# A transformer stack in float32 on one core: x, tables and results kept feature-major, modulation summed by VectorE

## What is computed

```python
for i in range(2):                                   # first block
    x = x + 0.5 * swiglu(rms_norm(x, g[i, 0]), w_gate_up[i, 0], w_down[i, 0])
    x = x + attention_i(rms_norm(x, g[i, 1]))
    x = x + 0.5 * swiglu(rms_norm(x, g[i, 2]), w_gate_up[i, 1], w_down[i, 1])
for i in range(2):                                   # second block
    shift_x, scale_x, gate_x = split(silu(c) @ w_mod[i] + b_mod[i], 3)
    shift_c, scale_c, gate_c = split(silu(c_ctx) @ w_mod[i] + b_mod[i], 3)
    hx = rms_norm(x, norm_g[i]) * (1 + scale_x) + shift_x
    hc = rms_norm(ctx, norm_g[i]) * (1 + scale_c) + shift_c
    ox, oc = mixer_i(hx, hc)
    x = x + gate_x * (ox @ w_o[i])
    if i == 0: ctx = ctx + gate_c * (oc @ w_o[i])
return rms_norm(x, final_g)
```

## Time and profile before

| | us |
|---|---|
| median of 3 runs (lowest, highest) | 3031.51 (3030.82, 3036.52) |
| the profiled execution, its own time | 3030.34 |
| its span, first to last instruction | 3028.5 |
| mean granted TensorE clock, of full speed | 0.972 |
| TensorE matmul busy | 2870.4 |
| VectorE / ScalarE / GpSimd busy | 1529.5 / 1147.8 / 110.4 |
| moved by DMA | 234.27 MB, 77 GB/s over the span |

### The profile page before, as it was taken

How to read it: one execution, slowest core, us unless ns; L and a number is a source line. 1 busy time by engine, 2 the same in 40 slices (tenths; PEclk the granted TensorE clock), 3 DMA queues, 4 the chain that set the end, 5 groups by cost and what they waited for, 6 DMA issues and landing times.

```text
span 3028.5 us, 38808 instructions
## 1 busy us (share of the span) xinstructions
PE 2870.4 (95%) x14416; PEld 2334.9 (77%) x14416; DVE 1529.5 (51%) x2151; ACT 1147.8 (38%) x1799; POOL 110.4 (4%) x108
## 2 busy tenths in 40 slices
PE   7999999998999999999987899999999997999987
PEld 2588888887888888888866788887788886878876
DVE  2244426665544335442456444424566666367774
ACT  2323215555323224222354332223455555245452
POOL 1000000000000000000011000000101000010100
PEclk9999999999999999999998899999999998999998
DMA  8433322122333233333301133332111110111111
GB/s 306 153 93 99 99 97 60 45 62 56 98 97 97 97 97 88 99 93 103 92 28 29 49 94 101 91 105 75 49 42 42 35 42 21 56 42 29 43 29 63
DMA packets 333666, 234.27 MB, mean 77 GB/s; under 512 B 6952, under 2 KB 308112, under 8 KB 333584
## 3 DMA queue, kind: packets, MB, share of 16 engines
q1 hardware_dynamic: 332672, 231.63, 25.4%
q0 software_dynamic: 912, 1.53, 0.2%
HBM read 231.04 MB, written 2.10 MB: 77 GB/s over the span
## 4 chain that ended last, share of the span: by engine, by line
PE 88%; DVE 5%; ACT 4%; issue 2%; DMA 0%; POOL 0%; ACTq 0%; SPq 0%; DVEq 0%; POOLq 0%
PE ps L439 24%; PE ps L441 24%; PE ps L440 23%; PE ps L732 3%; PE ps L708 2%; PE ps L1067 2%; PE ps L1204 2%; PE ps L956 1%; PE ps L1042 1%; ACT apr L1837 1%; PE ps L835 1%; PE ps L839 1%; PE ps L920 1%; PE ps L1184 1%; DVE tmp L488 1%
## 5 line engine op out<-in xcount | busy, mean ns | idle before, releaser
L439 PE MATMUL ps<-act_h,wl 128*128 128x512 f32 x2224 | 891.5, 401 | 3.6 <-DVE act_l L2037 2.3
L441 PE MATMUL ps<-act_h,wh 128*128 128x512 f32 x2224 | 868.1, 390 | 0.0
L440 PE MATMUL ps<-act_l,wh 128*128 128x512 f32 x2224 | 867.3, 390 | 0.0
L434 DVE TENSOR_TENSOR wl<-raw,wh 128x1024 fp32r<-128x1024 f32 x382 | 461.1, 1227 | 526.5 <-ACT wh L430 521.7
L430 ACT ACTIVATE wh<-raw 128x1024 fp32r<-128x1024 f32 x382 | 392.5, 1051 | 420.8 <-PE ps L441 347.8
L439 PEld LDWEIGHTS ps<-act_h,wl 128*128 128x128 f32 x2224 | 418.7, 188 | 96.1 <-issue 10.6
L440 PEld LDWEIGHTS ps<-act_l,wh 128*128 128x128 f32 x2224 | 419.1, 188 | 89.9 <-issue 7.9
L441 PEld LDWEIGHTS ps<-act_h,wh 128*128 128x128 f32 x2224 | 418.2, 188 | 89.4
L439 PE MATMUL ps<-h_h,wl 128*128 (+1 forms) x704 | 277.4, 394 | 0.0
L441 PE MATMUL ps<-h_h,wh 128*128 (+1 forms) x704 | 276.0, 392 | 0.0
L440 PE MATMUL ps<-h_l,wh 128*128 (+1 forms) x704 | 273.2, 388 | 0.0
(11 more groups left out here) (339 smaller groups left out, 3805.7 us busy)
## 6 DMA issues: line engine op xcount, KB each, us to landing
raw<-in_ffn_w_gate_up SPq DMA_DIRECT2D x176, 512.0 KB, 4.0
raw<-in_ffn_w_down SPq DMA_DIRECT2D x88, 512.0 KB, 3.7
mod_raw<-in_w_mod SPq DMA_DIRECT2D x12, 2048.0 KB, 8.0
raw<-in_a_w_in SPq DMA_DIRECT2D x32, 512.0 KB, 4.1
raw<-in_sb_w_in SPq DMA_DIRECT2D x24, 512.0 KB, 3.9
raw<-in_b_w_in SPq DMA_DIRECT2D x20, 512.0 KB, 4.0
raw<-in_w_o SPq DMA_DIRECT2D x16, 512.0 KB, 4.0
raw<-in_sw_w_in SPq DMA_DIRECT2D x10, 512.0 KB, 4.0
```

The lines of the kernel that those rows point to most:

```text
L434: dve.tensor_tensor(wl[:, slot, :], raw[:, slot % RAWS, :], f32(wh[:, slot, :]), ALU.subtract).then_inc(lo_done[slot], 1)
L439: pe.matmul(bank, w_lo, r_hi, start=start, stop=False, skip_group_check=skip)
L440: pe.matmul(bank, w_hi, r_lo, start=False, stop=False, skip_group_check=skip)
L441: return pe.matmul(bank, w_hi, r_hi, start=False, stop=stop, skip_group_check=skip)
```

## The change

All transposes at the two ends go, by laying the arrays out on the host.

- x and ctx come feature-major, one contiguous 2 KB run for each partition and tile. SP issues first one DMA for `columns` (128 x 430: gains, b_mod, sinks, lambda vectors, frequencies), then the eight tiles of x, `kf`, `krows`, and then the FFN weights. The setup stage's transposes, copies, zeroing and the 17 small DMAs are gone.
- Each engine's work for the first tiles stands in `first_norm`: split of slot 0, then act_h/act_l tile by tile as x lands, split of slot 1, squares of x, the copy of `kr`.
- The mod stage is gone. w_mod comes as 96 chunks of 128 x 512 (output feature on the partition, half of the 1024 inputs along the row), issued on GpSimd's queue into two buffers (one of them in xc's space). GpSimd's queue also loads silu's arguments, broadcast to all partitions. For each chunk DVE runs two tensor_tensor_reduce (multiply, sum along the row), one for c and one for c_ctx, into `mpart`. 48 chunks are summed in each of the first two FFNs: 3 in each pass of the gate/up loop from the second on, 1 behind each of 18 `split_lo` of the down projection. DVE's loops of those two FFNs are unrolled. ACT takes the silu of the broadcast rows in the first pass of each.
- Lambda and the other small constants are worked out between the two loops of the first FFN (`constants` on DVE, `lambda_exponentials` on ACT), and `modulation` (7 small operations) at the same place of the fourth FFN.
- ctx is loaded by GpSimd's queue after the last chunk; its sum of squares is formed in the out stage of sw.
- At the end each of the eight tiles of `yt` is stored by its own 256 KB DMA on SP's queue as soon as it is written; the transposes and copies are gone.

Of the two functions named `first_norm` below, the first is ScalarE's, the second VectorE's; `modulation` is GpSimd's, `modulated` and `two` are VectorE's.

```diff
         def _(sp):
+            sp.dma_start(columns[:, :], a["columns"]).then_inc(columns_in, 16)
+            for k in range(KT):
+                sp.dma_start(x[:, k, :], a["x"][:, k, :]).then_inc(x_in[k], 16)
+            sp.dma_start(kf[:, :], a["shape_table"][:, 0:N_F * P]).then_inc(const_in, 16)
+            sp.dma_start(krows, a["shape_table"][:, N_F * P:]).then_inc(const_in, 16)
...
-            sp.wait_ge(rows_out, 8)
-            sp.dma_start(y_out[0].rearrange("(b p) d -> p b d", p=P), yrows[:, :, :]).then_inc(out_sem, 16)
-            sp.wait_ge(out_sem, 16)
+            for k in range(KT):
+                sp.wait_ge(xf_done, START + 8 * stages[-2].n["xf"] + k + 1)
+                sp.dma_start(y_out[:, k, :], yt[:, k, :]).then_inc(out_sem, 16)
+            sp.wait_ge(out_sem, 16 * KT)
...
+            def modulation(half_):
+                pool.wait_ge(mod_used, START + half_ * MOD_CHUNKS // 2)
+                for v, name in enumerate(("c_2", "c_ctx_2")):
+                    pool.dma_start(mod_silu[:, v, :], a[name][:, half_ * SEQ:(half_ + 1) * SEQ].to_broadcast([P, SEQ])
+                                   ).then_inc(mod_row_in, 16)
+                for i in range(half_ * MOD_CHUNKS // 2, (half_ + 1) * MOD_CHUNKS // 2):
+                    if i > 1:
+                        pool.wait_ge(mod_used, START + i - 1)
+                    pool.dma_start(mod_w[i % 2], a["w_mod_2"][:, i, :]).then_inc(mod_in[i % 2], 16)
...
+            def first_norm(st):
+                split_hi(act, *half(st.following, 0))
+                for k in range(KT):
+                    act.wait_ge(x_in[k], 16)
+                    act.activation(act_h[:, k, :], x[:, k, :], ACT.Identity,
+                                   scale=vec[:, st.gain + k:st.gain + k + 1]).then_inc(xhi_done, 1)
+                split_hi(act, *half(st.following, 1))
+                for n in range(KT):
+                    square(act, stages[0], n)
+                act.wait_ge(const_in, 16 * 2)
+                act.activation(kr[:, :, :].rearrange("p a b -> p (a b)"), krows, ACT.Copy).then_inc(consts_done, 1)
...
+            def first_norm(st):
+                split_lo(dve, *half(st.following, 0))
+                for k in range(KT):
+                    dve.wait_ge(x_in[k], 16)
+                    dve.nop().then_inc(xup_done, 1)
+                    gained_lo(st, k)
+                split_lo(dve, *half(st.following, 1))
+                for n in range(KT):
+                    add_square(dve, stages[0], n)
+                dve.wait_ge(consts_done, 2)
...
+                def modulated(n):
+                    i = f * MOD_CHUNKS // 2 + n
+                    if n == 0:
+                        dve.wait_ge(mod_silu_done, f + 1)
+                    dve.wait_ge(mod_in[i % 2], 16 * (i // 2 + 1))
+                    dve.wait_ge(mod_used, START + i)
+                    for v in range(2):
+                        last = dve.tensor_tensor_reduce(mod_w[i % 2] if v else mod_prod, mod_w[i % 2], mod_silu[:, v, :],
+                                                        1.0, 0.0, ALU.mult, ALU.add, mpart[:, f, n, v:v + 1])
+                    last.then_inc(mod_used, 1)
+
+                def two(i, extra):
                     split_lo(dve, *half(st, 2, i))
                     split_lo(dve, *half(st, 3, i))
                     gate_scaled(0, i)
                     up_scaled(0, i)
+                    if extra:
+                        modulated(3 * i - 3)
                     gated(0, i)
                     split_lo(dve, *half(st, 4, i))
                     h_lo(0, i)
+                    if extra:
+                        modulated(3 * i - 2)
                     gate_scaled(1, i)
                     split_lo(dve, *half(st, 5, i))
                     up_scaled(1, i)
+                    if extra:
+                        modulated(3 * i - 1)
                     gated(1, i)
                     h_lo(1, i)
...
+                if f == 0:
+                    constants()
+                if f == 3:
+                    modulation()
+                if f < 2:
+                    for t in range(2, 24):
+                        split_lo(dve, *half(st, 2 * FT + t))
+                        if t < 20:
+                            modulated(28 + t)
```

More of the change, by code:

```diff
@@ L167, in ffn @@
         plan.stage("ffn", lead=2 * FT + FT, layer=layer, j=j, count=("ffn", "res"))
-    plan.stage("setup", count=("res", "cres"))
-    plan.stage("mod")
+    plan.stage("setup", count=("res",))
     ffn(0, 0)
@@ L178, in make_plan @@
     plan.stage("sw", lead=2, fixed=2, times=4)
-    plan.stage("out", lead=8, w="sw", count=("res",))
+    plan.stage("out", lead=8, w="sw", count=("res", "cres"))
     ffn(1, 1)
@@ L215, in build_program @@
     w_down = [[tiled(a["ffn_w_down"][l, j]) for j in range(2)] for l in range(2)]
-    w_mod = [tiled(a["w_mod_2"][l]) for l in range(2)]
     w_sb_in, w_sw_in = tiled(a["sb_w_in"][0]), tiled(a["sw_w_in"][0])
@@ L665, in _ @@
                         pool.memset(f32(t[:, :, :]), 0.0).then_inc(B.zero, 1)
+                if st.kind == "ffn" and st.n["ffn"] < 2:
+                    modulation(st.n["ffn"])
                 if st.kind == "sw":
@@ L1320, in out_projection @@
                                 ctx_args=(ps[:, 4 + t, 0:CTX], actc_h, actc_l) if st.ctx else None)
-            def end():
-                pe.wait_ge(xf_done, START + 8 * stages[-1].before["xf"])
-                for b in range(NBLK):
-                    for k4 in range(2):
-                        transposes(2 * b + k4, lambda k: yt[:, 4 * k4 + k, b * P:(b + 1) * P],
-                                   4).then_inc(etr_done, 1)
-            for st in stages:
-                if st.kind == "setup":
-                    setup()
-                elif st.kind == "mod":
-                    modulation(st)
-                elif st.kind == "norm":
+            for st in stages:
+                if st.kind == "norm":
                     norm(st)
@@ L1400, in norm @@
                     if st.before["res"] == 1:
[L1401 to L1402 removed]
+                        first_norm(st)
                     return
@@ L1430, in norm @@
                         act.activation(dst[:, k, :], src, ACT.Copy).then_inc(xhi_done, 1)
-            def modulation(st):
-                for n in range(MOD_LOADS):
-                    act.wait_ge(mod_used, START + n + 1)
-                    act.activation(mod_rows[0:2, n * SEQ:(n + 1) * SEQ], ps[0:2, 2 + n % 4, :],
-                                   ACT.Copy).then_inc(mod_copied, 1)
-                for t in range(2):
-                    split_hi(act, *half(st, t))
             def ffn(st):
@@ L2042, in norm @@
                     if st.before["res"] == 1:
-                        for k in range(KT):
-                            gained_lo(st, k)
+                        first_norm(st)
                     return
```

284 lines of the change are left out of this document (119 added, 165 removed).

## The result

The changed kernel takes 2943.88 us (median of 4 runs, 2934.53 to 2944.93), the kernel before 3034.02 beside it on the same chip (3030.82 to 3038.26). The ratio is 0.9695, with a 95% interval of 0.9671 to 0.972: faster by 90 us. The prediction was 2924.4 with a range of 2918 to 2935. It was **wrong**: the sign and most of the gain are there, but the kernel is 19.5 us slower than forecast. Two later executions, one with a spacer of 192 bytes (3273.92 us at a granted clock of 0.83) and one of the kernel before beside it (11497.76 us), lay far outside all others and stand in no ratio.

What follows compares the result with a forecast made beforehand. TensorE's matmuls bound the middle, so only the two ends could gain: 3028.5 - 98.0 - 10.4 + 0.8 + 0.5 = 2921.4 us of span, 2923.2 profiled, 2924.4 as median; range 2918 to 2935.

Steps and rivals of the forecast that it cites:

- The first matmul: Start: TensorE's first projection begins at 17.65 us (15.6 to 19.7) instead of 115.67, 98.0 us less.
- the first rival: Start: raw 0 shares the rate or x lands late; first matmul at 20 to 22, time 2927 to 2931; chance 0.11.
- The third term, from landing to matmul: Start: ACT's and DVE's splits, then gained_lo to the first matmul, 1.07, 1.18 and 0.90, together 3.15 us.
- The clock at the start: First projection: the same 6 us at 1.2 GHz as before, no difference in time.
- The mean: First norm: mean of squares ready 11.7 us behind the first matmul, mean 0.1 later; 0.8 us more (0 to 2).
- VectorE's work and the chunks: First two FFNs: 192 sums of 0.7 us, 134 us hidden; chunks land in 4 us against 9.6; nothing on the path.
- The second and third rivals: First two FFNs: chunks land late, 2930 to 2949 us, chance 0.09; slow sums make VectorE the bound, 192 t - 387, chance 0.02.
- The rule of the shared port: GpSimd's queue: VectorE in a port-sharing mode blocks GpSimd's DMA descriptors; chunks could land several us late, against 9.6 us allowed.
- Constants behind the loop: Between the first FFN's loops: constants and exponentials delay the slots' splits, 11.8 against 11.0; 0.5 us more (0 to 3), once.
- The middle of the kernel: From first L439 to last yt: the prediction is wrong if this is longer than 2899.1 + 1.3 us.
- The median: Whole kernel: median of the runs 1.2 us above the profiled execution, 2923.2 to 2924.4.
- The end: Last norm and stores: the end comes at 3018.1 on the old timeline instead of 3028.5, 10.4 us less.

Runs made afterwards that it cites:

- spacer of 192 bytes: Kernel before with 192 unused bytes a partition ahead of the overlaid tensors (h_h at 138112): 3028.5 us, ratio 0.9987.
- The early load: Changed kernel with ScalarE's first table load asked for before its first wait: 2943.22 us, ratio 0.971.
- The spacers: Unused tensors ahead of the overlaid ones: kernel before with 32, 64, 192 bytes, 3044.28, 3048.27, 3028.5 us; changed kernel with 32, 160 bytes, 2926.57, 2945.24 us.
- The 32 bytes: Changed kernel with an unused tensor of 32 bytes a partition ahead of the overlaid tensors (h_h at 138624): 2926.57 us, ratio 0.9651.
- the same bytes in the kernel before: Kernel before with the 32-byte unused tensor ahead of the overlaid tensors (h_h at 137952): 3044.28 us, ratio 1.0045.
- the 64 bytes: Kernel before with 64 unused bytes a partition ahead of the overlaid tensors (h_h at 137984): 3048.27 us, ratio 1.0037.

## Why the prediction was wrong, and where it was right

**The first matmul (17.65, 15.6 to 19.7): mis-sized.** It came at 23.55. In kind this is the first rival, a late start because raw 0 shares the rate, but it came beyond even that rival's 20 to 22. Two terms failed. Raw 0 landed at 19.06, not at 14.5: I had summed the rates of the kernel before to 4.67 MB, but those belonged to another queue. In the changed kernel the same sum over its own rates reaches 4.67 MB only at 16.7 us, and raw 0 lands 2.3 later, while raw 1 shares the rate. GpSimd's queue did not begin at about 5 us as I read from the earlier trace rows, where its first issue had waited for VectorE, but at 2.40, and had issued its megabyte by 4.7. Holding GpSimd back gave 3.2 of these 4.6 us; for the rest the low rate from 3 to 6 us remains, cause open. Second, "ACT's first table load, and columns, come long before" was half wrong: columns did, but the table load stood behind the wait for raw 0, for 1.28 us. The early load moved it to 3.24 and showed this. The third term, from landing to matmul, was right: 3.15 forecast, 23.55 - 20.35 = 3.20 measured. The sum is 4.6 + 1.3 + 0.05 = 5.9 us.

**The clock at the start.** I expected 6 us of slow matmuls. They took 0.63 us each until 27.1 and 0.40 from then, 3.6 us behind the first. It was worth nothing, since the mean waits for the squares, not for TensorE. The record of the granted clock shows 1.00 in these 3.6 us, where the earlier trace rows show 0.50; the durations are the better witness here.

**The mean (+0.8): right.** 35.2 is 11.65 behind the first matmul, forecast 11.8.

**VectorE's work and the chunks: right.** A sum takes 685 ns (forecast 0.7), with another starting 0.61 us later; chunks landed in a median of 3.3 us (forecast 4) and GpSimd waited for VectorE, never VectorE for a chunk. Only the first two took as long as the sign of being wrong (9.6 and 10.0 us, in the crowded start); they were first used at 61.5 and cost nothing, and of the others none took over 7.7. No TensorE wait in the first two FFNs but the mean's, 1.6 us. Leaving the work out changed 0.5 us of the total. The second and third rivals did not happen; the third's price was tested with four times the sums: its place and its waits held (114 us), and its sum fell 34 us or more short of the 165 measured, for want of the slower clock.

**The rule of the shared port.** The transfers of w_mod were issued from GpSimd's queue in 0.54 us each, all 96 alike, and landed in 3.3 us in the median while VectorE was busy 209.5 of the first FFN's 364.2 us. The Trainium skill, SBUF — State Buffer, in its part on the two sides of SBUF, gives the slowing for VectorE's faster modes; the trace agrees that float32 products and sums don't bring it about, and no run here shows the other case.

**Constants behind the loop (+0.5): nothing.** Lambda and its exponentials ended at 273.5 and the slots were split by 277.7; TensorE had no wait there. The estimate of 0 to 3 held its lower end.

**"The middle of the kernel" (2899.1 + 1.3 us): this step failed, and its cause was missing from the sum.** I had taken every matmul that the diff doesn't touch to keep its duration. The tensors h_h and h_l and the attention outputs moved by 672 bytes, and 2496 matmuls became 4.1 ns longer on the mean: 10.3 us. The four FFNs' stretches are 9.2 us longer (2.7 + 2.2 + 2.0 + 2.3), 8.7 of it these matmuls; the other stretches, with the output projections and the varying clock of the sliding-window stage in them, add up to -1.4, which gives the 7.8. No rival had this mechanism. The spacers show it directly, in both kernels and both directions. By the prediction's own measure, from the first matmul to the last yt, the middle is 2906.6 us where 2900.4 was the limit.

**The median (+1.2 above the profiled execution): failed too.** It is 9.35 above, since the profiled execution had a sliding-window stage of 241.2 us and most have 249 to 251. In the kernel before the profiled execution had 244.3, so a usual execution of the changed kernel loses 5 to 7 us here. Why the changed kernel is mostly at the long value is not settled. The 32 bytes gave 248.4, the same bytes in the kernel before 243.7, the 64 bytes 250.1 and the 192 bytes 246.8, so it follows neither the change nor the address alone.

**The end (-10.4): right in kind, 1.7 too small.** The end is 8.0 us behind the start of yt, before 19.1: 11.1 us. The stores landed in 2.1 us, near the lower bound of 2.0, where I had taken a value between the bounds: 0.7 us. The other 0.95 is luck: the last mean ran at a granted clock of 1.00 instead of 0.50 in this profile, which the change doesn't bring about.

All terms: 5.75 + 7.3 - 1.7 + 8.15 = 19.5 us.

## What to carry to other kernels

When a change adds or drops a buffer, list where every later tensor now starts, and compare the duration of unchanged matmuls by operand in both profiles before looking for a cause in the new work; where they differ, try a spacer of a few dozen bytes. At the start of a kernel the order in the queue decides: the operand with the longest chain behind it (land, split, split again) goes first, and a rate taken from a kernel with other transfers is not to be summed for it. An engine's table load belongs ahead of its first wait, and the price of a wait in a row of matmuls is the wait and the slower clock behind it.

## What the runs showed of the hardware

- A float32 matmul of 128 x 512 takes 389 ns when its moving tensor starts 128 bytes behind a multiple of 256, and 388 to 399 elsewhere (remainders 0, 96, 192 and 224 seen); over 2496 matmuls that is up to 16 us of 2944. The weights started 128 behind a multiple of 256 in all kernels, so whether the start itself or its place relative to the weights counts wasn't told apart. The Trainium skill, SBUF — State Buffer, in "Operand start alignment", asks only for a multiple of the element size and says of its own runs that they "timed nothing"; all of these starts are allowed by it, and not equally fast.
- One program spends 241.2 or 251.1 us in the same stage from one execution to the next, at a granted clock of 0.90 or 0.85, in a stage where TensorE is busy for about 81% of the time. In the FFNs, where it is busy for 99.9%, the stretches of the changed kernel repeat to 0.2 us.
- Two matmuls of the last mean took 2.08 us at a granted clock of 0.50 and 1.13 us at 1.00, with the same instructions before them.
- With TensorE waiting 38 times in two loops, the granted clock there fell from 1.00 to 0.95 and 0.94, and TensorE's busy time grew by 51 us beside 114 us of waits.
- Eight issues on SP's queue took 5.40 us beside GpSimd's first issues and 4.20 without them.
